# The first RMS norm of a three-layer block is applied after the product instead of before it, its first weight chunk comes in two transfers, and two modulation pieces move to another phase

## The reference, cut to what matters

```
h    = rmsnorm(x, attn_pre_norm)          # x / sqrt(mean(x^2) + eps) * gain, per token
proj = h @ w_in                           # 1956 columns
... sliding-window attention with sinks and a relative bias; forgetting attention;
c_q, c_kv, k_rope = latent columns of proj
qm = rmsnorm(c_q) @ w_uq ; kv = rmsnorm(c_kv) @ w_ukv ; rope on 32 columns
mixed = concat(rmsnorm(out_a), rmsnorm(out_b), rmsnorm(out_c))
x = x + rmsnorm(mixed @ w_out)
h = rmsnorm(x, ffn_pre_norm) ; u = conv(h @ w_up) ; ...

# layers 2 and 3
m = silu(c) @ ada_w + ada_b               # 6 modulation vectors for each layer
```

## Time and profile before

| | |
|---|---|
| median of 3 runs | 1077.59 us (1077.09 to 1077.86) |
| profiled execution | 1082.86 us, span 1081.1 us |
| TensorE busy | 1043.8 us, 97% of the span |
| VectorE busy | 814.4 us, 75% |
| ScalarE busy | 589.3 us, 55% |
| GpSimd busy | 150.8 us, 14% |
| chain that ended last | TensorE 72%, VectorE 19%, ScalarE 5% |
| DMA | 227.25 MB, 210 GB/s mean |

### The profile page before, as it was taken

One profiled execution on the slowest core, in us unless ns is written; L12 is line 12 of the kernel. 1 busy time (PEld: TensorE's weight loads), 2 busy tenths in 40 slices (PEclk: granted clock), 3 DMA queues, 4 the chain that ended last, 5 costly groups with the idle time before them and its releaser, 6 DMA issues.

```text
span 1081.1 us, 20330 instructions
## 1 busy us (share of the span) xinstructions
PE 1043.8 (97%) x7901; PEld 991.1 (92%) x7901; DVE 814.4 (75%) x1392; ACT 589.3 (55%) x1015; POOL 150.8 (14%) x162
## 2 busy tenths in 40 slices
PE   7999998999999999999999999999999999999998
PEld 6987798999888897899999999988899999999997
DVE  5767689999998987587999788785558666684443
ACT  5687467666446675665434445433466456544442
POOL 0000033333201100023111011200000112111010
PEclk9999999999999999999999999999999999999999
DMA  9642235777795533256998787445334635674550
GB/s 371 230 156 79 81 147 198 285 275 278 275 380 217 175 138 118 104 210 235 366 349 334 276 318 299 157 165 186 118 127 147 215 137 198 251 296 137 171 174 39
DMA packets 33684, 227.25 MB, mean 210 GB/s; under 512 B 3747, under 2 KB 4044, under 8 KB 9932
## 3 DMA queue, kind: packets, MB, share of 16 engines
q1 hardware_dynamic: 33164, 223.63, 56.0%
q0 software_dynamic: 448, 2.63, 0.6%
HBM read 225.19 MB, written 2.63 MB: 211 GB/s over the span
## 4 chain that ended last, share of the span: by engine, by line
PE 72%; DVE 19%; ACT 5%; issue 3%; DMA 1%; DVEq 0%; SPq 0%; ACTq 0%
PE psum L1384 17%; PE psum L1386 17%; PE psum L1385 17%; DVE w_lo L2090 7%; DVE arena L2194 4%; PE psum L1749 3%; PE psum L1751 3%; PE psum L1750 3%; PE psum L1449 2%; PE psum L1452 2%; PE psum L1451 2%; ACT w_hi L762 2%; DVE arena L2347 1%; DVE arena L2387 1%; DVE h_lo L2355 1%
## 5 line engine op out<-in xcount | busy, mean ns | idle before, releaser
L2090 DVE TENSOR_TENSOR w_lo<-raw,w_hi 128x1024 fp32r<-128x1024 f32 (+1 forms) x342 | 398.4, 1187 | 158.9 <-ACT w_hi L762 147.0
L762 ACT ACTIVATE w_hi<-raw 128x1024 fp32r<-128x1024 f32 (+1 forms) x342 | 335.7, 997 | 237.6 <-PE psum L1386 179.9
L1384 PE MATMUL psum<-h_hi,w_hi 128*128 128x256 f32 (+1 forms) x1144 | 330.1, 289 | 13.8 <-DVE w_lo L2090 7.1
L1385 PE MATMUL psum<-h_lo,w_hi 128*128 128x256 f32 (+1 forms) x1144 | 324.3, 283 | 0.0
L1386 PE MATMUL psum<-h_hi,w_lo 128*128 128x256 f32 (+1 forms) x1144 | 323.1, 282 | 0.0
L1384 PE MATMUL psum<-hid_hi,w_hi 128*128 128x256 f32 (+1 forms) x952 | 272.1, 286 | 2.8 <-DVE w_lo L2090 2.4
L1385 PE MATMUL psum<-hid_lo,w_hi 128*128 128x256 f32 (+1 forms) x952 | 270.0, 284 | 0.0
L1386 PE MATMUL psum<-hid_hi,w_lo 128*128 128x256 f32 (+1 forms) x952 | 269.7, 283 | 0.0
L1384 PEld LDWEIGHTS psum<-h_hi,w_hi 128*128 128x128 f32 x1144 | 217.6, 190 | 18.8 <-DVE w_lo L2090 9.2
L1385 PEld LDWEIGHTS psum<-h_lo,w_hi 128*128 128x128 f32 x1144 | 218.4, 191 | 0.7 <-issue 0.7
L1386 PEld LDWEIGHTS psum<-h_hi,w_lo 128*128 128x128 f32 x1144 | 218.5, 191 | 0.0
(11 more groups left out here) (266 smaller groups left out, 1185.8 us busy)
## 6 DMA issues: line engine op xcount, KB each, us to landing
arena<-in_ada SPq DMA_DIRECT2D x48, 1024.0 KB, 6.2
raw<-in_gu SPq DMA_DIRECT2D x44, 1024.0 KB, 5.9
raw<-in_ret_in SPq DMA_DIRECT2D x24, 1024.0 KB, 4.7
raw<-in_up SPq DMA_DIRECT2D x22, 1024.0 KB, 4.8
raw<-in_dn SPq DMA_DIRECT2D x32, 704.0 KB, 4.2
raw<-in_qkv SPq DMA_DIRECT2D x12, 1024.0 KB, 4.8
raw<-in_down SPq DMA_DIRECT2D x11, 1024.0 KB, 7.2
raw<-in_ret_o SPq DMA_DIRECT2D x8, 1024.0 KB, 4.8
```

The lines of the kernel that those rows point to most:

```text
L762: nc.scalar.activation(w_hi[chunk % SPLIT_SLOTS][:, a:b], raw[chunk % RAW_SLOTS][:, a:b], ACT.Copy)\
L1384: nc.tensor.matmul(out, w[0], hc, start=start, stop=False, skip_group_check=True)
L1385: nc.tensor.matmul(out, w[0], lc, start=False, stop=False, skip_group_check=True)
L2090: tt(w_lo[s][:, a:b], raw[chunk % RAW_SLOTS][:, a:b], w_hi[s][:, a:b].bitcast(F32), ALU.subtract)\
```

## The change

- x is multiplied by the gain alone and split into `Z_PRE` (ScalarE with a scale for the high part, VectorE for the low), in the free part of `hid_hi` and `hid_lo`. LAT0, LAT1 and KA multiply this. Their sums in PSUM are multiplied by the factors `rbc_pre` as VectorE takes them out (`leave_scaled`), in place of ScalarE's copies.
- The squares, the sums and the factors are made beside these products. The true h (scaled, rounded and split, eight tiles) is made after, for QA0 and the chunks behind it, between the other work of ScalarE and VectorE.
- Chunk 0 comes in two transfers, with a semaphore for the first. cols goes ahead of the second half of x, and onehot and ident behind chunk 1.
- The bias band's matmul stands in LAT1, and its copy on ScalarE behind the root.
- The fill at the start is 34 matmuls and not 16; the other fills of the first norm go.
- The two ada pieces of w_in move to w_out. SP waits, behind the load of w_out's last chunk, until all tiles of the group norms are made, and then loads both. ScalarE makes silu(cond) behind its split of w_out's last chunk, with the root's table loaded again after it. VectorE reduces both pieces behind its split of that chunk and ahead of the first chunk of up.

```diff
-ADA_STEPS = [("w_in", 10, lambda c: int(c in (KA, QA0))), ("up", 22, ...
+ADA_STEPS = [("w_out", 4, lambda c: int(c in (1, 2))), ("up", 22, ...
+        Z_PRE = (hid_hi[:, (FT - DT) * S:], hid_lo[:, (FT - DT) * S:])
+        rbc_pre = a1["pT"][:, 0:S]
...   SP
-            sp.dma_start(cols[:, :], dram["cols"]).then_inc(cols_in, 16)
-            sp.dma_start(onehot, dram["onehot"]).then_inc(onehot_in, 16)
-            sp.dma_start(ident[:, :], dram["ident"]).then_inc(ident_in, 16)
+                if k == 0:
+                    sp.dma_start(cols[:, :], dram["cols"]).then_inc(cols_in, 16)
...
+                    if chunk == 0:
+                        sp.dma_start(raw[0][:, 0:n // 2], src[:, 0:n // 2]).then_inc(first_in, 16)
+                        sp.dma_start(raw[0][:, n // 2:n], src[:, n // 2:n]).then_inc(raw_in[0], 16)
+                        return
...
+                    if ph.name == "w_out" and step.j == ph.n - 1:
+                        sp.wait_ge(h_tiles, tiles_before(FFNPRE))
...   ScalarE
-            for k in range(0, DT, 2):
+            act.wait_ge(cols_in, 16)
+            for k in range(DT):
                 if k % 4 == 0:
                     act.wait_ge(x_in[k // 4], 16)
+                cut = slice(k * S, (k + 1) * S)
+                nc.scalar.activation(Z_PRE[0][:, cut], x[:, cut], ACT.Identity, scale=col("pre", k)).then_inc(pre_hi, 1)
+                if k == 5:
+                    hi(0, ahead=0)
+            hi(0, ahead=1)
+            for k in range(0, DT, 2):
                 square(PRE, k, 2)
+            hi(LAT1)
+            warm_root(PRE)
+            root(PRE)
             act.wait_ge(band_ps, 1)
             nc.scalar.activation(band, tra[0][0:8, 0:BAND], ACT.Copy).then_inc(band_ready, 1)
...
+            hi(KA)
+            act.wait_ge(rbc_ready, nth(PRE))
+            nc.scalar.activation(rbc_pre, spread_bank(PRE, 0), ACT.Copy).then_inc(pre_rbc, 1)
+            for k in range(DT):
+                round_tile(PRE, k)
+                if k == 1:
+                    hi(QA0)
+                    act.wait_ge(lin_free[0], 1)
+                    act.wait_ge(lin_free[1], 1)
+                    square(LATENT, 0, 3)
+                if k == 6:
+                    root(LATENT)
+                    hi(ROWS0)
...
             hi(out0 + 3)
+            act.wait_ge(cond_in, 16)
+            nc.scalar.activation(cond_silu, cond_silu, ACT.Silu).then_inc(cond_ready, 1)
+            warm_root(FFNPRE)
...   TensorE
-            keep_busy(16)
+            keep_busy(34)
...
-            features(ph, LAT0, bank_free(0), 2, DT, first_tiles=(h_tiles, 0))
-            features(ph, LAT1, bank_free(1), 2, DT)
+            features(ph, LAT0, bank_free(0), 2, DT, Z_PRE, first_tiles=(pre_tiles, 0), hooks={14: lambda: sums(PRE)}, by_tile=False)
+            features(ph, LAT1, bank_free(1), 2, DT, Z_PRE, hooks={2: bias_band, 8: lambda: spread(PRE)})
...
-            features(ph, QA0, bank_free(3), 2, DT, hooks={11: lambda: spread(LATENT)})
+            features(ph, QA0, bank_free(3), 2, DT, first_tiles=(h_tiles, 0), hooks={11: lambda: spread(LATENT)})
...   VectorE
+            for k in range(DT):
+                ...
+                dve.wait_ge(pre_hi, k + 1)
+                stt(Z_PRE[1][:, cut], x[:, cut], col("pre", k), Z_PRE[0][:, cut].bitcast(F32), ALU.mult, ALU.subtract).then_inc(pre_tiles, 1)
+                if k == 5:
+                    lo(0, ahead=0)
+            lo(0, ahead=1)
             ... the squares are added ...
-            norm_h(PRE, lambda: lo(0))
+            lo(LAT1)
+            dve.wait_ge(ident_in, 16)
+            rstd(PRE)
+            lo(KA)
...
+            dve.wait_ge(pre_rbc, 1)
+            leave_scaled(LAT0, (a1["lat"][:, 0:512], 0))
+            scale_pre(0)
+            for k in range(DT):
+                if k + 1 < DT:
+                    scale_pre(k + 1)
+                dve.wait_ge(hh_ready, k + 1)
+                tt(hl[:, cut], e0["y"][:, cut], hh[:, cut].bitcast(F32), ALU.subtract).then_inc(h_tiles, 1)
+                if k == 1:
+                    leave_scaled(LAT1, (a1["lat"][:, 512:768], 0), (a1["kr"], S))
+                if k == 2:
+                    lo(QA0)
+                if k == 4:
+                    leave_scaled(KA, (a1["ka"], 0))
+                if k == 5:
+                    rstd(LATENT)
             lo(ROWS0)
...
-            pieces("w_in", Step(QA0))
...
             lo(out0 + 3)
+            dve.wait_ge(cond_ready, 1)
+            pieces("w_out", Step(1))
+            pieces("w_out", Step(2))
             lo(PH["up"].chunk0)
```

More of the change, by code:

```diff
@@ L120 @@
 ADA_PIECES = 24
-ADA_STEPS = [("w_in", 10, lambda c: int(c in (KA, QA0))), ("up", 22, lambda c: int(c >= 7 and c % 2)),
+ADA_STEPS = [("w_out", 4, lambda c: int(c in (1, 2))), ("up", 22, lambda c: int(c >= 7 and c % 2)),
              ("down", 11, lambda c: int(c < 10)), ("gu0", 22, lambda c: int(4 <= c <= 19)), ("dn0", 16, lambda c: c % 2),
@@ L627, in one @@
                     if ph.name == "w_in" and step.j == 1:
+                        sp.dma_start(ident[:, :], dram["ident"]).then_inc(ident_in, 16)
+                        sp.dma_start(onehot, dram["onehot"]).then_inc(onehot_in, 16)
+                    if ph.name == "w_in" and step.j == 3:
                         sp.dma_start(cond_silu, dram["cond"]).then_inc(cond_in, 16)
@@ L752, in hi @@
                 at = (lambda f: f(chunk)) if step is None else (lambda f: step.n(lambda c: f(ph.chunk0 + c + 1)))
-                act.wait_ge(raw_in[chunk % RAW_SLOTS], at(lambda k: 16 * (k // RAW_SLOTS + 1)))
+                if chunk or ahead != 0:
+                    act.wait_ge(raw_in[chunk % RAW_SLOTS], at(lambda k: 16 * (k // RAW_SLOTS + 1)))
                 for half, (a, b) in enumerate(of.halves(c)):
@@ L756, in hi @@
                         continue
+                    if chunk == 0 and half == 0:
+                        act.wait_ge(first_in, 16)
                     if chunk >= SPLIT_SLOTS:
@@ L841, in _ @@
             qscale, mla_scale = HD ** -0.5, (HD + ROPE) ** -0.5
[L842 to L855, removed]
             nc.scalar.activation(warm[:, LATENT:LATENT + 1], ones[:, 0:1], ACT.Exp)
@@ L1506, in _, with bias_band @@
             pe.wait_ge(busy_ready, 1)
-            keep_busy(16)
+            keep_busy(34)
             pe.wait_ge(cols_in, 16)
-            pe.wait_ge(onehot_in, 16)
-            nc.tensor.matmul(tra[0][0:8, 0:BAND], col("rel", 0, 8, BUCKETS + 1), onehot, start=True, stop=True).then_inc(band_ps, 1)
             pe.wait_ge(ones_filled, 1)
-            norm(PRE, 0, 8, 4)
+            def bias_band():
+                pe.wait_ge(onehot_in, 16)
+                nc.tensor.matmul(tra[0][0:8, 0:BAND], col("rel", 0, 8, BUCKETS + 1), onehot, start=True, stop=True).then_inc(band_ps, 1)
             def bank_free(unit):
@@ L1524, in features @@
                 order = [(b, k) for b in range(nb) for k in range(kt)]
-                if first_tiles is not None:
+                if first_tiles is not None and by_tile:
                     order.sort(key=lambda o: o[1])
@@ L1537, in features @@
                     ins = three(bank[:, b * S:(b + 1) * S], (whi[:, cut], wlo[:, cut]), rhs[0][:, t], rhs[1][:, t],
-                                start=n == 0, stop=whole and n == blocks - 1)
+                                start=n == 0, stop=n == blocks - 1)
                     if at in (cut2 - 1, blocks - 1):
@@ L2259, in pair_to_mixed, with leave_scaled, scale_pre @@
                 nc.vector.tensor_copy(a1["mixed"][:, k:k + S], att[0][:, 0:S]).then_inc(att_out, 1)
[L2261 to L2266, removed]
+            def leave_scaled(c, *todo):
+                dve.wait_ge(half_done, 2 * (c + 1))
+                for to, at in todo:
+                    n = to.shape[1] // S
+                    ins = tt(v3(to, n), v3(lin[UNIT_OF[c] % 2][:, at:at + n * S], n), over(rbc_pre, n), ALU.mult)
+                leave(ins, UNIT_OF[c])
+            dve.wait_ge(pre_rbc, 1)
+            leave_scaled(LAT0, (a1["lat"][:, 0:512], 0))
+            def scale_pre(k):
+                cut = slice(k * S, (k + 1) * S)
+                stt(e0["y"][:, cut], x[:, cut], col("pre", k), rbc_pre, ALU.mult, ALU.mult).then_inc(t_ready, 1)
+            scale_pre(0)
+            for k in range(DT):
+                if k + 1 < DT:
+                    scale_pre(k + 1)
+                cut = slice(k * S, (k + 1) * S)
+                dve.wait_ge(hh_ready, k + 1)
[4 more added lines that the diff above has]
+                    lo(QA0)
+                if k == 4:
+                    leave_scaled(KA, (a1["ka"], 0))
+                if k == 5:
+                    rstd(LATENT)
             lo(ROWS0)
```

21 lines of the change are left out of this document (7 added, 14 removed).

## The result

The changed kernel takes 1090.86 us (median of 4 runs, 1088.72 to 1094.97) against 1077.72 beside it (1077.09 to 1083.63): a ratio of 1.0103, 95% interval 1.0063 to 1.0142. The forecast was slower by 2.6 us, 1080.2 and at most 1083.6. The sign was right, the size was not: it is 9 to 13 us.

What follows compares the result with a forecast made beforehand. TensorE held 72% of the chain of waits and VectorE 19%; a loss of 5.85 us at the end of attention less a net lead of 3.3 gave +2.6 on 1077.59, so 1080.2 us, range 1075.4 to 1083.6.

Steps and rivals of the forecast that it cites:

- The move, step by step: End of attention: up's first chunk lands late, row sums 4.95 us late, slow transposes add 0.9; loss 5.85.
- Rival 2: End of attention: load behind SP's wait hidden, only VectorE's two pieces count, 3.1 us late; 1076.7 us, chance 0.08.
- The net lead of 3.3 us: Opening through attention: lead of 4.0 us less 0.7 for clock dips, bounds 1.5 and 4.5.
- The second half of the working: Opening, after the factors (PSUM at 21.35): VectorE's list bounds, its tile 8 at 35.3, first scores at 41.1.
- rival 1: Opening: TensorE, not VectorE, orders 21 to 41 us, so QA0 ends 6.9 early; 1075.6 us, chance 0.14.
- a lump of 0.7: Opening to first scores: 0.7 us taken off the lead for clock dips, between 0 and 3.2.
- The rest of the lead: Attention: first scores 3.7 us early, lead carried through as 4.0 us, bounds 2.4 and 5.
- Rival 3: Clock falls twice early, before 11 and before 41 us, and the end's restart costs 2.5; 1082.6 us, chance 0.13.
- Rival 4: Bias chain late: bias lands at 46 us where VectorE asks at 41, lead -1; 1085 us, chance 0.05.
- the 5.3 us: Whole kernel: the profiled execution, 1082.86 us, stood 5.3 above the median of 1077.59; the same offset was kept.
- The pieces in w_in: Before the scores: first ada piece's removal gains nothing more; the second's 2.5 us puts VectorE's splits and scores 4.8 early.
- The signs: Listed trace marks to check, among them w_out's transposes about 1 us later than 139.5, granted clock 0.5 after them.

Runs made afterwards that it cites:

- e2: Kernel before with its old opening, only the two ada pieces, Silu and SP's wait moved to w_out: 1088.43 us, ratio 1.0065 to the kernel before.
- e5: The changed kernel measured again, unaltered: 1091.33 us, ratio 1.0081 to the kernel before.
- e7: The changed kernel with 64 fill matmuls at the start in place of 34: ratio 1.0068 to the kernel before.
- e13b: e7 with the spread of the first norm's factors behind three blocks of LAT1, not eight: ratio 1.0067 to the kernel before.
- e8: The changed kernel with its new opening, but both ada pieces back in w_in: 1084.34 us, ratio 1.0031 to the kernel before.
- e9: e8 with 64 fill matmuls in place of 34: 1081.06 us, ratio 1.0005 to the kernel before.
- e6: The changed kernel, but SP loads the first chunks of up before its wait and the pieces: 1088.8 us, ratio 1.0059 to the kernel before.
- e12b: e9 with the spread of the first norm's factors behind three blocks of LAT1, not eight: ratio 1.0007 to the kernel before.
- e1: The kernel before measured once more against itself, with a second trace: 1082.4 us, ratio 1.0002.
- e10: Kernel before, pieces moved: up loaded ahead of SP's wait, one piece behind VectorE's split of up's first chunk, one behind the row diagonals: 1083.11 us, ratio 1.0019.
- e11: The changed kernel's opening with 64 fills and the ada pieces placed as in e10: ratio 1.0034 to the kernel before.
- e14b: Kernel before with 21, 6, 13 and 14 fill matmuls in the opening in place of 16, 0, 8 and 4: 1078.89 us, ratio 0.9964.
- e4: Kernel before with its old opening, the two ada pieces moved to chunks 5 and 6 of up: ratio 1.0055 to the kernel before.
- e3: The changed kernel with the two ada pieces at chunks 5 and 6 of up and no wait in SP's queue: ratio 1.0058 to the kernel before.

## Why the prediction was wrong

- **The move, step by step: right.** The load behind SP's wait, the two pieces, the late split, squares and row sums: 4.95 forecast, 4.85 in e2; slow transposes 0.9, measured 0.91. In after the same steps take 6.15: its first chunk of up lands 10.2 us after issue (10.2 to 10.3 in e5, e7 and e13b too) and in e2 8.9, with the same five transfers queued. Why this differs no run shows. Rival 2 (load hidden) is refuted by 5.75 us of idle time on that load.
- **The net lead of 3.3 us: this step failed.** At the first scores after has 0.7 of it, at w_out nothing, and in e8 the opening costs 1.6 to 5.0 us. The second half of the working is right: from ScalarE's copy of the factors to the first scores 19.7 us were forecast, and 24.39 to 44.11 is 19.7. VectorE's list is the bound there, as forecast, and its tile 8 comes at 38, so rival 1 is out. But the factors come 3.0 late, and all of it is on TensorE's line. The first block is 1.34 late: the first half of chunk 0 was there at 9.66 and not at 8.55, which makes its split 1.1 late, and TensorE starts 0.3 behind VectorE's end. Another 1.5 are the matmuls at the lower clock from 12.8 to 16.0, and 0.2 lie in between. The stand ahead of that fall was put at 1.1 to 3 us and was 3.92, because the 34 fills took 5.81 us and not up to 7.3 and the first block was late. The clock was treated as a lump of 0.7 taken off at the end; it stood in the middle of the chain, ahead of the sums, the spread and everything behind them. e9 and e7 take the fall away and the spread comes 1.0 and 0.8 earlier; in e6 it is absent with the same code, and spread and first scores come 1.95 earlier.
- **What e12b and e13b add.** The forecast took the place of the spread (behind eight blocks) as given. By its own numbers TensorE came to it about 1.5 us after its diagonals, and in after it is 2.6. Moving it gives about 0.3 at the first scores in e13b and nothing in e12b.
- **The rest of the lead was lost in attention.** It was carried on unchanged. There the clock sets the time, in all 16 profiles: from the first scores to w_out they take 66.6 to 67.3 us without any time at 0.50 between 40 and 112 us (e1, e9, e10, e11, e12b, e13b, e14b), 68.1 to 68.4 with 3.4 us of it (before, e2, e4), 69.3 with 6.8 (after, e3, e5, e6), 71.0 with 10.2 (e8) and 72.6 with 13.7 (e7). So 1 us at 0.50 costs about 0.4 here, and after lost 0.9 against before by it. All five profiles with the new opening and 34 fills have 6.8 us or more, and four of the five with 64 fills none. So the fill and this stretch, some 80 us later, go together; by what, and why e7 is different, stays open. Rival 3 was the nearest to what came: the clock does fall early, at the fourth real matmul, but not again before the scores, and its price was still too small.
- **Rival 4: wrong.** VectorE's rows show no wait for the bias; the chain's third transfer is issued at 34.05.
- **From the profiled execution to the median.** I took the 5.3 us between them as a constant. It was one draw: later sets of the kernel before have medians of 1081.3 to 1082.4 and single runs from 1077.7 to 1084.9. In the profiled pair the change costs 6.0, in the two sets of timed runs 9 to 11 by the ratios and 10 to 13 by the medians. A range built on 5.3 us of offset was too tight at its upper end.
- **The pieces in w_in.** I gave the leaving of the first no price at TensorE's first scores and let the second count behind them. By e10 against e1 that was about right: 0.2 at the first scores, 0.5 at w_out. The late places cost 2.7 (e10) to 5.8 us (e2).
- **A slip.** The signs end with transposes "5.9 - 4 = about 1 us later"; the difference is 1.9. They came 6.4 us later.

## What to carry over

Work that stands beside idle time is free only where it stands: price the place where it goes by what the engine does there (here VectorE is busy 31.8 of the 38 us from 127 to 165 in before), and read in the issuing queue what a new wait is put ahead of. A lead at the start counts only if the next thing in every engine's order can use it; follow the one value that all wait for (here the factors) on each engine's line. Before a restructuring of an opening, try the cheap thing: fill TensorE up to its first real instruction; here this alone gave 3.9 us (2.3 to 5.4 by the interval), of which 1.6 to 1.9 are seen in the opening, while the whole change gave a loss.

## What the runs showed of the hardware

Summed over the windows of 2 us, the time at the granted clock of 0.50 is 13.6 us in before, 20.5 in e1 (the same kernel), 23.9 in after, 6.8 in e14b and 3.4 in e9 and e12b. Beside busy matmuls it costs up to half of itself: the matmuls from 12.8 to 16.0 in after take 0.21 each and not 0.12, 1.5 us more in all, and in attention 1 us of it costs about 0.4. Whether the clock falls behind a given stand differs between executions. TensorE stands 1.78 us before 189.64 in before and 1.78 before 192.55 in e8. In before the clock stays up behind it, in e8 it falls (windows of before, then of e8):

```profile
190.00:192.00 2.00, 2.00 (x19) 1.00 0.93 389
```
```profile
192.00:194.00 2.00, 1.45 (x8) 0.75 0.81 270
```

In the opening, stands of 3.92 us (after), 4.42 (e5), 3.80 (e3) and 2.56 (e8) had matmuls 0.21 apart at the first block or a few matmuls behind it, and one of 2.85 (e6) did not.

Runs of one kernel differ by 5 to 11 us, where nine or more were timed. With the new opening the slow ones are those with the lower mean granted clock (the correlation of time and clock, -1 for a strict relation and 0 for none, is -0.93 in the 12 runs of e9, -0.82 in e12b, -0.78 in e8, -0.71 in e11). With the old opening this is not so: 0.1 over the 79 runs of before that stand beside the others, 0.13 in e10, -0.18 in e14b. There the cause stays open, and the record of the clock is also less sure: in the opening of before the matmuls from 17.78 to 22.2 are 0.21 apart while the record says 1.00; in e1, the same code, it says 0.50 from 10 to 22. There the spacing of the matmuls is the surer reading.
